# mLSTM and differential heads in another order, gates taken as tanh from PSUM

## The reference

```
q,k,v,gates,o,dq,dk,dv,p8,p9 = split(u @ w_in)
h   = mLSTM forward over q,k,v + mLSTM backward          # 4 heads, values of 256
a   = rmsnorm(h, per head of 256) * m_norm * sigmoid(o)
s1,s2 = softmax(dq1 dk1 / 8), softmax(dq2 dk2 / 8)       # 8 heads, keys of context and latents
b   = rmsnorm((s1 - lam * s2) @ dv, per head of 128) * d_norm * (1 - lam_init)
y   = (sigmoid(p8) * (a @ w_a) + sigmoid(p9) * (b @ w_b)) @ w_o
x   = x + g1 * y
x   = x + g2 * experts(modulate(rmsnorm(x)))
```

## Time and profile before

| | us |
|---|---|
| median of 3 runs (2455.96 to 2459.93) | 2459.82 |
| profiled execution, its own time | 2460.78 |
| its span | 2459.0 |
| PE busy in the span (matmuls) | 2365.6 (96%) |
| PE busy with weight loads, beside the matmuls | 1773.3 (72%) |
| DVE busy | 775.4 (32%) |
| ACT busy | 435.0 (18%) |
| first matmul of mLSTM head 0 | 1228.91 |
| first matmul of the differential scores | 1329.35 |
| first product with w_a | 1421.51 |
| first expert product ends, SP issues the next expert load | 1526.84 |

### The profile page before, as it was taken

The page is one execution under the profiler, slowest core; times in us unless marked ns, Lnnn a source line. Parts: engine busy times, 40 slices in busy tenths (PEclk is TensorE's granted clock), DMA queues, the critical chain, the costliest instruction groups (busy, mean ns, idle before and its releaser), DMA issues.

```text
span 2459.0 us, 31834 instructions
## 1 busy us (share of the span) xinstructions
PE 2365.6 (96%) x13140; PEld 1773.3 (72%) x13140; DVE 775.4 (32%) x1889; ACT 435.0 (18%) x1038; POOL 0.2 (0%) x4
## 2 busy tenths in 40 slices
PE   8799999999989999999998899999999999999998
PEld 7688888888878888888876587555555555555554
DVE  6843374210444412000244643221212211112212
ACT  4242202010232212000023422111111111111111
POOL 0000000000000000000000000000000000000000
PEclk9999999999999999899999999999999999999999
DMA  6134476665224442232122165999999999999996
GB/s 256 38 120 149 150 270 245 231 224 184 90 102 140 152 154 103 86 120 86 67 71 86 52 261 194 406 427 429 428 429 428 428 428 428 428 428 428 429 428 272
DMA packets 56631, 606.94 MB, mean 247 GB/s; under 512 B 6304, under 2 KB 6688, under 8 KB 7488
## 3 DMA queue, kind: packets, MB, share of 16 engines
q1 hardware_dynamic: 56544, 605.72, 61.7%
HBM read 604.65 MB, written 1.05 MB: 246 GB/s over the span
## 4 chain that ended last, share of the span: by engine, by line
PE 85%; DVE 7%; DMA 6%; ACT 2%; issue 1%; SPq 0%; DVEq 0%; ACTq 0%
PE bank L568 27%; PE bank L1019 17%; PE bank L565 8%; PE bank L1045 7%; DMA ring<-in_experts 5%; PE bank L631 5%; PE bank L1012 3%; PE bank L557 3%; PE bank L582 2%; PE bank L980 2%; DVE arena L1567 2%; PE bank L992 1%; PE bank L734 1%; PE bank L642 1%; ACT arena L1318 1%
## 5 line engine op out<-in xcount | busy, mean ns | idle before, releaser
L568 PE MATMUL bank<-arena,ring 128*128 128x256 f32 x3296 | 717.8, 380 | 0.0
L568 PEld LDWEIGHTS bank<-arena,ring 128*128 128x128 f32 x3296 | 627.7, 191 | 85.6
L1019 PE MATMUL bank<-ring,arena 128*64 128x256 f32 x2048 | 235.1, 382 | 4.5 <-DMA ring<-in_experts 4.5
L1959 DVE TENSOR_SCALAR arena<-bank 128x256 f32<-128x256 f32 x64 | 27.2, 425 | 668.5 <-PE bank L1019 668.5
L1019 PE MATMUL bank<-arena 128*64 128x256 f32 x2048 | 235.1, 382 | 2.2 <-DMA arena<-in_experts 2.2
L1019 PEld LDWEIGHTS bank<-ring,arena 128*64 128x64 f32 x2048 | 141.4, 137 | 91.0 <-issue 18.3
L1019 PEld LDWEIGHTS bank<-arena 128*64 128x64 f32 x2048 | 141.3, 137 | 88.4 <-issue 18.6
L565 PE MATMUL bank<-ring,arena 128*128 128x256 f32 x896 | 196.2, 381 | 0.0
L565 PEld LDWEIGHTS bank<-ring,arena 128*128 128x128 f32 x896 | 171.4, 191 | 23.5
L631 PE MATMUL bank<-arena,ring 128*128 128x256 f32 x576 | 124.6, 379 | 0.0
L631 PEld LDWEIGHTS bank<-arena,ring 128*128 128x128 f32 x576 | 109.4, 190 | 14.9
(11 more groups left out here) (270 smaller groups left out, 1964.3 us busy)
## 6 DMA issues: line engine op xcount, KB each, us to landing
arena<-in_experts SPq DMA_DIRECT2D x96, 2048.0 KB, 24.6
ring<-in_experts SPq DMA_DIRECT2D x96, 2048.0 KB, 26.3
ring<-in_dense SPq DMA_DIRECT2D x186, 1024.0 KB, 4.7
con<-in_con SPq DMA_DIRECT2D x1, 1248.0 KB, 12.2
X<-in_x SPq DMA_DIRECT2D x1, 1024.0 KB, 4.8
arena<-in_cond SPq DMA_DIRECT2D x1, 1024.0 KB, 17.8
arena<-in_ctx SPq DMA_DIRECT2D x1, 1024.0 KB, 4.7
arena<-in_mmask SPq DMA_DIRECT2D x1, 1024.0 KB, 6.8
```

The source lines that it names most:

```text
L568: ins = nc.tensor.matmul(o, w[:, k, j * P:(j + 1) * P], src[:, k, :], start=(k == 0), stop=(k == KT - 1))
L1019: ins = nc.tensor.matmul(o, XGT[:, k, e * CAP:(e + 1) * CAP], w[:, k, :], start=False, stop=(k == KT - 1), skip_group_check=True)
```

## The change

On PE the four bodies of an mLSTM head (rows, scores, turn, values) become functions, and are called a head ahead of each other: the next head's rows go between a head's turn and its values, its scores behind the values, and a gate half stands between any two where one would wait for the other. The first gate half goes ahead of head 0. DVE waits for rows and scores separately. The first p9 half and the statistics of heads 0 to 2 go between turn and values of mLSTM head 3. In the differential loop the values of head h-1 go behind the scores of h+1, and the p9 half h+2 behind them; the turn of h comes last. DVE takes the maxima of h+1 before the division of h, ACT the exponentials of h+1 before the copies of h. On DVE the rotations go ahead of the copy of the dv unit.

The gates are read from PSUM by Tanh with scale 0.5 (sigmoid(x) = (1 + tanh(x / 2)) / 2), where they were copied and put through Sigmoid later; the factor 1/2 goes into the mLSTM norm's root (scale 4) and into g1 (MOD times 0.5), and the products become (gate + 1) * value in one instruction. The mLSTM norm's root for heads 0 and 1 is taken before the values of mLSTM head 3, for heads 2 and 3 after the last differential exponentials, from a copy in SBUF. The last statistics are split 3, 3, 2.

```diff
-        if h == 0:
+    def m_rows(h):
+        if h:
+            pe.wait_ge(sem("m_pt"), 2 * h)
+        else:
             pe.wait_ge(sem("rope"), 16)
-        else:
-            pe.wait_ge(sem("m_pt"), 2 * h)
-            pe.wait_ge(sem("m_out"), h)
-        for qt in range(2):
-            nc.tensor.matmul(banks[4 + qt][:, :], MQ[:, h, qt * P:(qt + 1) * P], MK[:, h, :],
-                             start=True, stop=True)
         for d in range(2):
             pick = ident[0:8, 4 * d + h:4 * d + h + 1].to_broadcast([8, P])
             ins = nc.tensor.matmul(banks[6 + d][:, :], pick, RT, start=True, stop=True)
+        ins.then_inc(sem("m_rows"), 1)
...
+    def m_scores(h):
+        if h:
+            pe.wait_ge(sem("m_out"), h)
+        for qt in range(2):
+            ins = nc.tensor.matmul(banks[4 + qt][:, :], MQ[:, h, qt * P:(qt + 1) * P], MK[:, h, :],
+                                   start=True, stop=True)
         ins.then_inc(sem("m_scores"), 1)
-        for n in range(4 * h, 4 * h + 3):
-            gate_half(n)
...
+    def m_turn(h):
...
-        gate_half(4 * h + 3)
+    def m_values(h):
...
+    def hm_stat(first, end):
+        for h in range(first, end):
+            for v in range(2):
+                pe.wait_ge(sem("hm_sq"), before("hm_sq") + 2 * h + v + 1)
+                ins = nc.tensor.matmul(banks[h // 2][:, (h % 2) * T:(h % 2 + 1) * T], C("mean256"), SQM[:, 2 * h + v, :],
+                                       start=(v == 0), stop=(v == 1))
+            if h % 2:
+                ins.then_inc(sem("hm_sum"), 1)
+    gate_half(0)
+    units_read(pe, "dv")
+    m_rows(0)
+    m_scores(0)
+    for n in range(1, 4):
+        gate_half(n)
+    for h in range(3):
+        m_turn(h)
+        gate_half(4 * h + 4)
+        m_rows(h + 1)
+        m_values(h)
+        gate_half(4 * h + 5)
+        m_scores(h + 1)
+        gate_half(4 * h + 6)
+        gate_half(4 * h + 7)
+    m_turn(3)
+    gb_half(0)
+    units_read(pe, "ga")
+    hm_stat(0, 3)
+    m_values(3)
...
-    d_scores(0)
-    units_read(pe, "ga")
...
-    ins.then_inc(sem("hm_sum"), 1)
-    gb_half(0)
-    for h in range(HEADS):
-        if h + 1 < HEADS:
-            d_scores(h + 1)
-            gb_half(h + 1)
+    def d_turn(h):
         if h == 0:
-            pe.wait_ge(sem("hm_root"), 2)
+            pe.wait_ge(sem("hm_root"), 1)
+            pe.wait_ge(sem("hm_kept"), 1)
...
+    def d_values(h):
         pe.wait_ge(sem("d_pt"), 2 * h + 2)
         if h:
...
-    pe.wait_ge(sem("d_exp"), 4 * HEADS)
-    do_stat(0, 6)
+    d_scores(0)
+    hm_stat(3, 4)
+    gb_half(1)
+    for h in range(HEADS):
+        if h + 1 < HEADS:
+            d_scores(h + 1)
+        if h:
+            d_values(h - 1)
+        if h + 2 < HEADS:
+            gb_half(h + 2)
+        d_turn(h)
+        if h == HEADS - 2:
+            pe.wait_ge(sem("d_exp"), 4 * HEADS)
+            do_stat(0, 3)
+    do_stat(3, 6)
+    d_values(HEADS - 1)
...
-            nc.scalar.copy((GO, GA)[n // 4][:, 2 * i + j, :], half_of(u, j)).then_inc(read_sem(u), 1)
+            nc.scalar.activation((GO, GA)[n // 4][:, 2 * i + j, :], half_of(u, j), ACT.Tanh, scale=0.5)\
+              .then_inc(read_sem(u), 1)
...
-        nc.scalar.copy(GB[:, n, :], banks[STAT][:, (n % 2) * T:(n % 2 + 1) * T]).then_inc(sem("gb_read"), 1)
+        nc.scalar.activation(GB[:, n, :], banks[STAT][:, (n % 2) * T:(n % 2 + 1) * T], ACT.Tanh, scale=0.5)\
+          .then_inc(sem("gb_read"), 1)
+    def hm_root(b, src):
+        nc.scalar.activation(RSM[:, 512 * b:512 * b + 512], src, ACT.Sqrt, bias=EPS_M, scale=4.0)\
+          .then_inc(sem("hm_root"), 1)
...
         raw_gate(2 * h)
+        raw_gate(2 * h + 1)
         for b in range(2):
             act.wait_ge(sem("m_tr"), 2 * h + b + 1)
             nc.scalar.copy(MPT[:, 2 * b:2 * b + 2, :], tiles(banks[6 + b][:, :], 2)).then_inc(sem("m_pt"), 1)
-        raw_gate(2 * h + 1)
+        if h == 3:
+            raw_gb(0)
+            act.wait_ge(sem("hm_sum"), 1)
+            hm_root(0, banks[0][:, :])
+            nc.scalar.activation(small[:, 123:124], EPS_COL, ACT.Exp)
...
-    d_exps(0)
-    raw_gb(0)
-    act.wait_ge(sem("hm_sum"), 1)
-    for b in range(2):
-        nc.scalar.activation(RSM[:, 512 * b:512 * b + 512], banks[b][:, :], ACT.Sqrt, bias=EPS_COL)\
-          .then_inc(sem("hm_root"), 1)
...
-            if h and b == 0:
...
-        if h + 1 < HEADS:
-            d_exps(h + 1)
-            raw_gb(h + 1)
+    def d_out(h):
...
-    def gate(name, dst):
-        for c in range(0, KT, 2):
-            nc.scalar.activation(dst[:, c:c + 2, :], dst[:, c:c + 2, :], ACT.Sigmoid).then_inc(sem(name + "_sig"), 1)
-
-    units_read(act, "ga")
-    act.wait_ge(sem("gb_read"), KT)
-    gate("go", GO)
+    d_exps(0)
+    act.wait_ge(sem("hm_sum"), 2)
+    nc.scalar.copy(RSM[:, 512:1024], banks[1][:, :]).then_inc(sem("hm_kept"), 1)
+    raw_gb(1)
+    for h in range(HEADS):
+        if h + 1 < HEADS:
+            d_exps(h + 1)
+        else:
+            act.wait_ge(sem("hm_kept"), 1)
+            hm_root(1, RSM[:, 512:1024])
+        if h:
+            d_out(h - 1)
+        if h + 2 < HEADS:
+            raw_gb(h + 2)
+        for b in range(2):
+            act.wait_ge(sem("d_tr"), 2 * h + b + 1)
+            nc.scalar.copy(DPT[:, 2 * b:2 * b + 2, :], tiles(banks[b][:, :], 2)).then_inc(sem("d_pt"), 1)
+    d_out(HEADS - 1)
...
-        act.wait_ge(sem("do_sum"), 1 if b < 3 else 2)
+        act.wait_ge(sem("do_sum"), (1, 2, 2, 3)[b])
...
-    gate("ga", GA)
-    gate("gb", GB)
...
-        take(26 + i, 27 + i)
...
-
+        take(26 + i, 27 + i)
...
-        dve.wait_ge(sem("m_scores"), h + 1)
+        dve.wait_ge(sem("m_rows"), h + 1)
...
+        dve.wait_ge(sem("m_scores"), h + 1)
...
+    def out_gated(c):
+        dve.wait_ge(sem("hm_normed"), c + 1)
+        unit_half(dve, FIRST_UNIT["go"] + c // 2, 2)
+        V.scalar_tensor_tensor(HM[:, c, :], GO[:, c, :], 1.0, HM[:, c, :], ALU.add, ALU.mult).then_inc(sem("a_out"), 1)
     d_max(0)
     for h in range(HEADS):
         b = h % 2
+        if h + 1 < HEADS:
+            d_max(h + 1)
...
-        if h + 1 < HEADS:
-            d_max(h + 1)
-        if h < 4:
+        if h < 2:
             root_turned(h)
-        elif h < 7:
-            for c in range(3 * (h - 4), min(3 * (h - 3), KT)):
-                out_normed(c)
+        elif h < 4:
+            out_normed(2 * h - 4)
+            out_normed(2 * h - 3)
+        elif h < 6:
+            out_gated(2 * h - 8)
+            out_gated(2 * h - 7)
+    for h in (2, 3):
+        root_turned(h)
+        for step in (out_normed, out_gated):
+            step(2 * h)
+            step(2 * h + 1)
...
+    me(V.tensor_scalar(MOD[:, 16:24, 0], MOD[:, 16:24, 0], 0.5, None, ALU.mult))
...
-    for c in range(KT):
-        dve.wait_ge(sem("hm_normed"), c + 1)
-        dve.wait_ge(sem("go_sig"), c // 2 + 1)
-        V.tensor_tensor(HM[:, c, :], HM[:, c, :], GO[:, c, :], ALU.mult).then_inc(sem("a_out"), 1)
...
-        dve.wait_ge(sem("ga_sig"), c // 2 + 1)
-        V.tensor_tensor(YM[:, c, :], GA[:, c, :], half_of(u, c % 2), ALU.mult).then_inc(read_sem(u), 1)
+        unit_half(dve, FIRST_UNIT["ga"] + c // 2, 2)
+        V.scalar_tensor_tensor(YM[:, c, :], GA[:, c, :], 1.0, half_of(u, c % 2), ALU.add, ALU.mult)\
+         .then_inc(read_sem(u), 1)
...
-        dve.wait_ge(sem("gb_sig"), c // 2 + 1)
-        V.tensor_tensor(t[:, c % 4, :], GB[:, c, :], half_of(u, c % 2), ALU.mult).then_inc(read_sem(u), 1)
+        dve.wait_ge(sem("gb_read"), c + 1)
+        V.scalar_tensor_tensor(t[:, c % 4, :], GB[:, c, :], 1.0, half_of(u, c % 2), ALU.add, ALU.mult)\
+         .then_inc(read_sem(u), 1)
```

More of the change, by code:

```diff
@@ L334, in build @@
         EPS_D = small[:, 96:97]
+        EPS_M = small[:, 97:98]
         RCOL = small[:, 98:100]
@@ L824, in _ @@
                     turned(1, 2 * (i - 2))
-            units_read(pe, "dv")
-            for h in range(4):
-                if h == 0:
+            def m_rows(h):
+                if h:
+                    pe.wait_ge(sem("m_pt"), 2 * h)
+                else:
                     pe.wait_ge(sem("rope"), 16)
-                else:
-                    pe.wait_ge(sem("m_pt"), 2 * h)
-                    pe.wait_ge(sem("m_out"), h)
-                for qt in range(2):
-                    nc.tensor.matmul(banks[4 + qt][:, :], MQ[:, h, qt * P:(qt + 1) * P], MK[:, h, :],
-                                     start=True, stop=True)
                 for d in range(2):
@@ L1319, in d_exps @@
                                          scale=SCALE_D, accum_out=DDEN[h % 2][:, i:i + 1]).then_inc(sem("d_exp"), 1)
-            d_exps(0)
-            raw_gb(0)
-            act.wait_ge(sem("hm_sum"), 1)
-            for b in range(2):
-                nc.scalar.activation(RSM[:, 512 * b:512 * b + 512], banks[b][:, :], ACT.Sqrt, bias=EPS_COL)\
-                  .then_inc(sem("hm_root"), 1)
-            for h in range(HEADS):
-                for b in range(2):
```

(9 more changed lines are left out.)

## The result

The changed kernel took 2436.60 us (median of 4 runs, 2431.17 to 2438.93) against 2459.88 (4 runs, 2455.96 to 2460.23): ratio 0.9906, 95% interval 0.9891 to 0.9921. It is 23.3 us faster; forecast were 30.4 with a range from 2423.5 to 2440.

The account below looks back on a forecast made before the run. PE, with its waits and half clock, was taken as the bound. Gains of 14.6 us up to differential scores 0 and 15.8 after, 30.4 in all, gave 2429.5 us (own range 2426 to 2432), full range 2423.5 to 2440.

Parts of the forecast that it names:

- rival A: At turn 6 the clock falls again (2.7 us), or waits return in six differential heads; 2432 to 2438 us, chance 0.23.
- Start: At the section's start, rotations first remove 3.14 us of idle PE and 5.15 us of half clock.
- mLSTM heads: PE's work sets each mLSTM head: 22.06 us from turn to turn, against 24.16 before.
- Differential heads: In the differential loop PE's work sets each iteration: 8.2 us, against 9.93 before.
- the turn's 0.5 us to spare: DVE's maxima and division chain end 0.5 us before the differential turn needs them, the tightest place.
- Path (a): Differential scores to end of exponentials: 6.9 us after the scores' start the next may go, 1.3 us to spare.
- Loop's end: From differential scores 7 to the first wa product: 15.0 us, including a 2.4 us wait for divisions.
- rival D: Longer waits before differential turns halve the clock and the loop runs at 1.2 GHz; 2502 us, chance 0.02.
- Tanh: On ACT, reading a gate by tanh takes 0.42 us, near the copy's 0.37, without a table switch from Exp.
- Rival B: Tanh needs another table than Exp: two 1.28 us loads a head, 3 us in six heads; 2433 us, chance 0.06.
- Carried 1:1: A gain in the section reaches the end whole, since the expert stream's start moves with PE.
- rival C: The expert stream starts no earlier, so gain is lost: 2445 us with half lost, 2460 with all; chance 0.05.

Follow-up runs that it names:

- e1: Changed kernel with only the start undone: rotations behind the dv copies, all four gate halves behind head 0's rows and scores; 2442.07 us, ratio 0.9937 to before.
- t1: The kernel before, unchanged, profiled once more for its tail; 2454.33 us in one run.
- t2: Changed kernel with three more PE instructions that do nothing, ahead of the w_out products; 2430.59 us, ratio 0.9892 to the kernel before.
- t4: The changed kernel, unaltered, run and profiled again; 2437.69 us, ratio 0.9895 to the kernel before.
- e2: Changed kernel with only the order of the mLSTM heads put back; 2446.26 us, ratio 0.9949 to the kernel before.
- t3: Changed kernel with 128 more PE instructions that do nothing, half a 16 KB fetch; 2475.41 us, ratio 1.0071 to the kernel before.
- e5: Changed kernel with Sigmoid straight from PSUM in place of Tanh and the factors of 1/2 out; 2437.36 us, ratio 0.9913 to the kernel before.
- e6: Changed kernel with gates copied as before, Sigmoid and its product behind the differential loop; 2438.09 us, ratio 0.9910 to the kernel before.
- e3: Changed kernel with only the order of the differential loop put back; 2449.32 us, ratio 0.9968 to the kernel before.

## Why the prediction was right, and by what it missed

The time lay in the range, 7 us above the likeliest value and outside its own range of 2426 to 2432. In part that is luck: 2436.60 falls among the times of rival A (2432 to 2438), whose mechanism, the clock at turn 6, brought only 1.7 us of the miss; the largest part stands in no rival. The steps of the sum inside the section came out within about half a us each where the clock held. Step by step:

- **Start** (8.3 us forecast). The 3.14 us of idle went, and PE ran on at 1.00. The clock's 5.15 us is not a fixed price: the same idle 3.19 us cost 5.15 in the first profile, some 3.4 in e1, and nothing in t1, where rows and scores ran at full speed (its section of 192.9 holds another fall of the clock, at 1343). The term is 3 to 8 us.
- **mLSTM heads** (22.06 us a head). 21.97. Turn 0 came 17.5 us behind dv's end, forecast 17.7. Differential scores 0 started 94.67 us behind it (forecast 95.2).
- **Differential heads** (8.2). 8.17 on average from scores 2 to scores 7, with the turn's 0.5 us to spare intact. Path (a) ended 6.95 behind its start, forecast 6.9.
- **Loop's end** (15.0 from scores 7). 15.1 in the profiles in which the clock held (e1, t2, t4), 16.5 to 16.8 where it fell (changed, e2, t3, e5). The gap before turn 6 was 2.17 us (1.97 in e5), between the 2.10 and 2.75 of the earlier trace rows, and it went both ways. The prediction read these two rows as a line between waits that lower the clock and waits that don't, and leaned on it against rival D; there is no such line. In t1, the same kernel as in the earlier trace rows, the wait of 2.10 us was followed by half speed (the scores took 3.36 for 1.99), and e2's 2.83 us were not. Rival A's price of 2.7 was 1.7. The whole section: forecast 165.3, measured 165.3 with the clock up and 167.0 without.
- **Tanh** (0.42). 0.37 us, as the copy, and no load stands between it and Exp. Rival B's switch costs 0.6 us by e5, not 3: the loads fit into ACT's gaps. A switch is 1.28 us, with 0.02 behind it, also where two a head follow each other; the 2.66 of the Trainium skill ("ScalarE: Activation LUTs", What ACT_TABLE_LOAD costs) was not seen.
- **Carried 1:1**. Through w_a, w_b, w_o and the expert stream it held: 101.6 us from w_a to the first expert product in both, 919.0 and 918.9 from there to the last table load, and the first expert load came 26.5 us earlier, so rival C is out. What failed is a term put at nothing without a reason: I took all that is unedited to cost what it cost. The edit left PE's program three instructions shorter. Behind the expert loop a fetch of instructions then lands in PE's pause, the first instructions start 1.8 us later, and the clock falls: 4.6 us in all.

In the two profiled executions the gain is 21.9 us (2460.78 to 2438.93), 8.5 short of 30.4: 4.6 behind the expert loop, 1.6 in the section (the clock at turn 6), and 2.3 in the first half, where the same code ran at the lower clock for longer. With the three instructions put back (t2) the median is 2430.59, and 2429.5 was forecast; but on that chip the kernel before took 2456.10, and t2's ratio of 0.9892 would be 2433.3 beside 2459.88, so this closeness proves nothing. What t2 shows is the 4.0 us at the end of its trace.

What is shown is that three PE instructions ahead of the expert loop decide whether the wait is there, that it is a wait for instructions, and which fetch it is. Why the fetches fall where they do is open; the added instructions stood in one place only, and only three lengths were tried (17192, 17195 and 17320 instructions), so the length of the program and the place of its later code are not told apart.

## What to carry to other kernels

When PE's waits are already short and each has the same releaser in every turn of a loop, count PE's work in a turn, lay the other engines' path beside it from the same start, and reorder until every path is shorter; such a sum came out within 1% here. Give the last pieces of filler work to the turns that have none, not to waits that something else covers. After any edit compare stretches that were not edited, the first instructions behind a loop above all: three instructions fewer cost 4.6 us here, as much as two mLSTM heads had gained (2 x 2.2), and a padded copy of the kernel told it.

## What the runs showed of the hardware that I had not expected

- Three PE instructions more, none of them doing anything, took 4.0 us off the end of the program (940.4 to 936.4 from the first expert product). By whole times this can't be told: t2's ratio is 0.9892 (0.9872 to 0.9911), those of the changed kernel 0.9906 and 0.9895. With 128 more the span was 37.1 us longer (2474.2 for 2437.1).
- A PE wait of one length was followed by the 1.2 GHz level in some executions and not in others: 3.19 us in two of three (before, e1; not t1), 2.83 not (e2), 2.75 in two of two (before, t1), 2.0 to 2.2 at turn 6 in four of eight (changed, e2, e5, t3; not in e1, e6, t2, t4), 2.10 before the scores of head 2 in one of two (t1, not before). The two longest in the section, 3.48 (e6) and 3.77 (e3), were followed by it. The waits of 3.2 to 4.1 us behind the expert loop were followed by it in all eight, those of 1.35 in none of five.
- The same first 1220 us of code ended up to 9.0 us apart from execution to execution (1221.5 to 1230.5), by how long the clock stayed at its lower level in them.
- Two table loads a head, 2.56 us of ACT's 8.2, changed the loop by 0.1 us a head.
